# New step lists for the differential-attention layers of a 6-layer transformer kernel

## What is computed

```python
def diff_attention(h, w_in, w_out, ..., sub_g, cos, sin, lambda_init):   # 8 heads, two maps of 64 each
    q, k, v = jnp.split(h @ w_in, [1024, 2048], axis=-1)                 # 256 x 3072
    q = apply_partial_rope(q, cos, sin) * 64 ** -0.5
    k = apply_partial_rope(k, cos, sin)
    s = einsum('bqhcd,bkhcd->bhcqk', q, k)                               # c = 0, 1
    p = softmax(where(causal, s, -inf), axis=-1)
    p = p[:, :, 0] - lam * p[:, :, 1]
    o = einsum('bhqk,bkhe->bqhe', p, v)
    return (rms_norm(o, sub_g) * (1.0 - lambda_init)).reshape(B, S, 1024) @ w_out
```

## Time and profile before

| | us |
|---|---|
| median of 3 runs | 1507.87 (1502.86 to 1507.88) |
| the profiled execution | 1507.24, span 1505.5 |
| TensorE busy in it | 1446.0 (96%), mean granted clock 0.985 |
| VectorE busy | 982.0 (65%) |
| ScalarE busy | 819.4 (54%) |
| mixer of the launch layer (us 11 to 137 of the span) | TensorE's products stand still five times for over 0.1 us |
| mixer of layer 4 (us 889 to 1007) | five times too |
| HBM read | 239.84 MB, 160 GB/s |

### The profile page before, as it was taken

How to read it: one execution, slowest core, us unless ns; L and a number is a source line. 1 busy time by engine, 2 the same in 40 slices (tenths; PEclk the granted TensorE clock), 3 DMA queues, 4 the chain that set the end, 5 groups by cost and what they waited for, 6 DMA issues and landing times.

```text
span 1505.5 us, 19084 instructions
## 1 busy us (share of the span) xinstructions
PE 1446.0 (96%) x7727; PEld 1225.4 (81%) x7727; DVE 982.0 (65%) x1416; ACT 819.4 (54%) x1325; POOL 41.8 (3%) x72
## 2 busy tenths in 40 slices
PE   7999999999999999999999999999999989899988
PEld 6777888888878888887888887778888877788787
DVE  6664665566647655693765567647655698858984
ACT  6675444355535443573543355755443558846883
POOL 3000000000000000000000000000000010102010
PEclk9999999999999999999999999999999999999998
DMA  9343455553434454443445454434454554424430
GB/s 294 116 165 113 168 206 185 185 200 119 168 112 168 172 214 173 155 154 111 169 169 210 181 189 161 168 112 168 169 212 179 175 147 137 168 101 157 144 112 29
DMA packets 119476, 242.13 MB, mean 161 GB/s; under 512 B 3050, under 2 KB 48924, under 8 KB 119388
## 3 DMA queue, kind: packets, MB, share of 16 engines
q1 hardware_dynamic: 117616, 237.25, 44.3%
q0 software_dynamic: 1408, 3.52, 1.0%
q10 hardware_dynamic: 364, 0.13, 0.0%
HBM read 239.84 MB, written 1.05 MB: 160 GB/s over the span
## 4 chain that ended last, share of the span: by engine, by line
PE 78%; DVE 9%; ACT 7%; DMA 4%; issue 1%; SPq 0%; ACTq 0%; DVEq 0%
PE pair L1164 16%; PE pair L1166 15%; PE pair L1165 15%; PE pair L1535 15%; PE pair L1537 8%; DVE wlo L1690 4%; ACT whi L695 3%; PE pair L1357 2%; PE pair L1258 2%; PE pair L1315 2%; DMA raw<-in_diff_w_in 1%; DVE xparts L1726 1%; DMA raw<-in_diff_w_out 1%; ACT xparts L727 1%; PE pair L1336 1%
## 5 line engine op out<-in xcount | busy, mean ns | idle before, releaser
L1690 DVE TENSOR_TENSOR wlo<-raw,whi 128x2048 fp32r<-128x2048 f32 (+2 forms) x240 | 506.3, 2146 | 84.5 <-ACT whi L695 83.7
L695 ACT ACTIVATE whi<-raw 128x2048 fp32r<-128x2048 f32 (+2 forms) x240 | 416.6, 1782 | 90.0 <-DMA raw<-in_mlp_w_down 27.7
L1535 PE MATMUL pair<-xparts,whi 128*128 128x512 f32 x1024 | 260.8, 394 | 7.3 <-DVE xparts L1726 7.1
L1164 PE MATMUL pair<-whi,xparts 128*128 128x512 f32 (+2 forms) x624 | 246.4, 395 | 16.8 <-DVE wlo L1690 8.3
L1164 PE MATMUL pair<-whi,ahi 128*128 128x512 f32 x640 | 254.1, 397 | 0.0
L1166 PE MATMUL pair<-whi,alo 128*128 128x512 f32 x640 | 250.9, 392 | 0.0
L1165 PE MATMUL pair<-wlo,ahi 128*128 128x512 f32 x640 | 250.7, 392 | 0.0
L1166 PE MATMUL pair<-whi,xparts 128*128 128x512 f32 (+2 forms) x624 | 240.6, 386 | 0.0
L1165 PE MATMUL pair<-wlo,xparts 128*128 128x512 f32 (+2 forms) x624 | 239.9, 385 | 0.0
L1535 PEld LDWEIGHTS pair<-xparts,whi 128*128 128x128 f32 x1024 | 184.2, 189 | 44.0 <-issue 6.9
L957 ACT ACTIVATE qkv<-pair 128x512 f32<-128x512 f32 x64 | 38.2, 597 | 274.0 <-PE pair L1537 274.0
(11 more groups left out here) (248 smaller groups left out, 1414.5 us busy)
## 6 DMA issues: line engine op xcount, KB each, us to landing
raw<-in_mlp_w_up SPq DMA_DIRECT2D x32, 2048.0 KB, 8.7
raw<-in_mlp_w_down SPq DMA_DIRECT2D x32, 2048.0 KB, 7.5
raw<-in_diff_w_in SPq DMA_DIRECT2D x22, 1024.0 KB, 7.2
raw<-in_w_in SPq DMA_DIRECT2D x10, 2048.0 KB, 7.8
raw<-in_moba_w_in SPq DMA_DIRECT2D x12, 1024.0 KB, 6.2
raw<-in_diff_w_out SPq DMA_DIRECT2D x4, 2048.0 KB, 7.7
raw<-in_w_uq SPq DMA_DIRECT2D x4, 1152.0 KB, 5.8
raw<-in_moba_w_out SPq DMA_DIRECT2D x2, 2048.0 KB, 8.4
```

Of the source, the lines that this page charges most:

```text
L695: act.activation(whi[:, s, cols], raw[:, s, cols], ACT.Copy).then_inc(*t["hi_split"].one())
L1164: pe.matmul(dst, x_hi, w_hi, start=first, stop=False)
L1535: pe.matmul(pair[f % 2][:, f // 2, :], w_hi[:, k, f * P:(f + 1) * P], xparts[:, k, :, :].rearrange("p a n -> p (a n)"), start=k == 0, stop ...
L1690: dve.tensor_tensor(wlo[:, s, cols], raw[:, s, cols], whi[:, s, cols].bitcast(FP32), ALU.subtract)\
```

## The change

The lists of the differential mixers are drawn anew. No step is added or removed, no step's own instructions change, and the order of blocks, loads and of the slots they use is as it was. `heads`, `scores`, `turn`, `mix` and `features` stand at other places between the eighths of `in` and `out`; on ScalarE and VectorE the two halves of a split are more often apart. TensorE's list in full, and of the other two the lines with the places that matter below (each code line stands 4 lines further down in the new file from L433 on):

```diff
@@ diff_tensor_steps
-            steps = part("in", 0, 0, 8) + part("in", 1, 0, 8) + [("heads", 0)] + part("in", 2, 0, 3)
-            steps += [("scores", 0)] + part("in", 2, 3, 8) + [("turn", 0)] + part("in", 3, 0, 2)
-            steps += [("scores", 1), ("heads", 1), ("mix", 0)] + part("in", 3, 2, 6) + [("turn", 1)] + part("in", 3, 6, 7)
-            steps += [("scores", 2)] + part("in", 3, 7, 8) + part("in", 4, 0, 4) + [("turn", 2), ("heads", 2), ("scores", 3)]
-            steps += part("in", 4, 4, 7) + [("mix", 1)] + part("in", 4, 7, 8) + part("in", 5, 0, 2) + [("turn", 3), ("features", 0)]
-            steps += part("in", 5, 2, 3) + [("scores", 4)] + part("in", 5, 3, 8)
-            steps += [("mix", 2), ("turn", 4), ("mix", 3), ("mix", 4), ("scores", 5), ("heads", 3)]
-            steps += [("features", 1), ("scores", 6)] + part("out", 0, 0, 2) + [("turn", 5)] + part("out", 0, 2, 3) + [("mix", 5)]
-            steps += part("out", 0, 3, 4) + [("scores", 7), ("turn", 6), ("features", 2), ("mix", 6)] + part("out", 0, 4, 6)
-            steps += [("turn", 7)] + part("out", 0, 6, 7) + [("mix", 7)] + part("out", 0, 7, 8) + part("out", 1, 0, 2)
-            steps += [("features", 3)] + part("out", 1, 2, 8)
+            steps = part("in", 0, 0, 8) + part("in", 1, 0, 7) + [("heads", 0)] + part("in", 1, 7, 8)
+            steps += part("in", 2, 0, 2) + [("scores", 0)] + part("in", 2, 2, 7) + [("turn", 0)] + part("in", 2, 7, 8)
+            steps += [("scores", 1)] + part("in", 3, 0, 4) + [("heads", 1)] + part("in", 3, 4, 6) + [("turn", 1)]
+            steps += part("in", 3, 6, 8) + [("mix", 0)] + part("in", 4, 0, 1) + [("scores", 2)] + part("in", 4, 1, 2)
+            steps += [("mix", 1)] + part("in", 4, 2, 3) + [("heads", 2)] + part("in", 4, 3, 4) + [("turn", 2)]
+            steps += part("in", 4, 4, 7) + [("scores", 3)] + part("in", 4, 7, 8) + part("in", 5, 0, 3) + [("turn", 3)]
+            steps += part("in", 5, 3, 4) + [("scores", 4)] + part("in", 5, 4, 5) + [("features", 0)]
+            steps += part("in", 5, 5, 6) + [("mix", 2)] + part("in", 5, 6, 8)
+            steps += [("mix", 3), ("heads", 3), ("turn", 4), ("features", 1), ("scores", 5)]
+            steps += [("mix", 4), ("scores", 6)] + part("out", 0, 0, 2) + [("turn", 5), ("mix", 5), ("scores", 7)]
+            steps += part("out", 0, 2, 4) + [("turn", 6), ("features", 2)] + part("out", 0, 4, 5) + [("mix", 6)]
+            steps += part("out", 0, 5, 6) + [("turn", 7)] + part("out", 0, 6, 7) + [("mix", 7)] + part("out", 0, 7, 8)
+            steps += part("out", 1, 0, 2) + [("features", 3)] + part("out", 1, 2, 8)
@@ diff_scalar_steps
...
-            steps += [("in_results", 1), ("scores", 0), ("split", 0), ("split", 1), ("turn", 0), ("in_results", 2)]
...
-            steps += [("split", 1), ("in_results", 5), ("turn", 4), ("outputs", 1), ("heads", 3), ("features", 1)]
...
+            steps += [("split", 1), ("scores", 0), ("in_results", 1), ("turn", 0), ("in_results", 2)]
...
+            steps += [("in_results", 5), ("outputs", 1), ("heads", 3), ("turn", 4), ("features", 1)]
...
@@ diff_vector_steps
...
-            steps += [("scores", 0), ("turn", 0), ("split", 0), ("split", 1), ("rope", 1), ("scores", 1)]
...
-            steps += [("features", 0), ("scores", 4), ("split", 0), ("turn", 4), ("split", 1), ("rope", 3)]
...
+            steps += [("split", 0), ("scores", 0), ("turn", 0), ("split", 1), ("scores", 1)]
...
+            steps += [("scores", 4), ("turn", 4), ("split", 1), ("features", 0), ("rope", 3)]
...
```

More of the change, by code:

```diff
@@ L414, in diff_scalar_steps @@
-            steps += [("outputs", 0), ("in_results", 4), ("turn", 3), ("features", 0), ("split", 0), ("scores", 4)]
-            steps += [("split", 1), ("in_results", 5), ("turn", 4), ("outputs", 1), ("heads", 3), ("features", 1)]
-            steps += [("scores", 5), ("split", 0), ("split", 1), ("turn", 5), ("scores", 6), ("outputs", 2)]
-            steps += [("turn", 6), ("scores", 7), ("features", 2), ("turn", 7), ("outputs", 3), ("features", 3)]
-            steps += [("out_results", 0)]
+            steps = [("in_results", 0), ("split", 0), ("split", 1), ("heads", 0), ("split", 0)]
@@ new lines, in diff_scalar_steps @@
+            steps += [("split", 1), ("scores", 0), ("in_results", 1), ("turn", 0), ("in_results", 2)]
+            steps += [("split", 0), ("scores", 1), ("split", 1), ("heads", 1), ("split", 0)]
+            steps += [("split", 1), ("turn", 1), ("in_results", 3), ("scores", 2), ("outputs", 0)]
+            steps += [("turn", 2), ("heads", 2), ("split", 0), ("in_results", 4), ("scores", 3)]
+            steps += [("split", 1), ("turn", 3), ("scores", 4), ("split", 0), ("features", 0)]
+            steps += [("in_results", 5), ("outputs", 1), ("heads", 3), ("turn", 4), ("features", 1)]
@@ L419, in diff_scalar_steps @@
+            steps += [("split", 1), ("scores", 5), ("split", 0), ("turn", 5), ("scores", 6)]
+            steps += [("outputs", 2), ("turn", 6), ("scores", 7), ("split", 1), ("turn", 7)]
+            steps += [("out_results", 0), ("features", 2), ("outputs", 3), ("features", 3)]
             return steps
         def diff_vector_steps():
-            steps = [("in_results", 0), ("in_results", 1), ("in_results", 2), ("in_results", 3), ("in_results", 4), ("in_results", 5)]
-            steps += [("split", 0), ("split", 1), ("rope", 0), ("heads", 0), ("split", 0), ("split", 1)]
@@ L425, in diff_vector_steps @@
-            steps += [("scores", 0), ("turn", 0), ("split", 0), ("split", 1), ("rope", 1), ("scores", 1)]
-            steps += [("heads", 1), ("turn", 1), ("split", 0), ("split", 1), ("scores", 2), ("rope", 2)]
-            steps += [("turn", 2), ("heads", 2), ("scores", 3), ("split", 0), ("split", 1), ("turn", 3)]
-            steps += [("features", 0), ("scores", 4), ("split", 0), ("turn", 4), ("split", 1), ("rope", 3)]
-            steps += [("scores", 5), ("heads", 3), ("features", 1), ("turn", 5), ("scores", 6), ("split", 0)]
@@ L430, in diff_vector_steps @@
-            steps += [("split", 1), ("turn", 6), ("scores", 7), ("turn", 7), ("features", 2), ("features", 3)]
-            steps += [("out_results", 0)]
+            steps = [("in_results", 0), ("in_results", 1), ("in_results", 2), ("in_results", 3), ("in_results", 4)]
+            steps += [("in_results", 5), ("rope", 0), ("split", 0), ("heads", 0), ("split", 1)]
+            steps += [("split", 0), ("scores", 0), ("turn", 0), ("split", 1), ("scores", 1)]
+            steps += [("rope", 1), ("split", 0), ("out_results", 0), ("turn", 1), ("split", 1)]
@@ new lines, in diff_vector_steps @@
+            steps += [("heads", 1), ("scores", 2), ("rope", 2), ("turn", 2), ("split", 0)]
+            steps += [("split", 1), ("heads", 2), ("scores", 3), ("turn", 3), ("split", 0)]
+            steps += [("scores", 4), ("turn", 4), ("split", 1), ("features", 0), ("rope", 3)]
+            steps += [("split", 0), ("heads", 3), ("scores", 5), ("features", 1), ("scores", 6)]
+            steps += [("turn", 5), ("split", 1), ("scores", 7), ("turn", 6), ("turn", 7)]
+            steps += [("split", 0), ("features", 2), ("features", 3), ("split", 1)]
```

3 lines of the change are left out of this document (removed).

## The result

| | before | after |
|---|---|---|
| median of 5 runs each, us | 1507.80 (1502.86 to 1507.88) | 1497.66 (1494.62 to 1499.20) |
| ratio, 95% interval | | 0.9948 [0.9932, 0.9964] |
| the profiled execution, us | 1507.24, span 1505.5 | 1497.7, span 1495.9 |
| mean granted clock in it | 0.985 | 0.987 |

The forecast was 1502.4 with a range from 1497.5 to 1507.5. With 0.52% it is just in the class "faster by over 0.5%" (chance 0.33), and its interval reaches down to 0.36%.

What follows compares the result with a forecast made beforehand. TensorE was taken as the bound, busy 1446.0 of 1505.5 us, so only its losses could be won. Launch layer -4.25 and layer 4 -0.6, together -4.85 from 1507.24, gave 1502.4 us, range 1497.5 to 1507.5.

Steps and rivals of the forecast that it cites:

- The launch copy: Launch layer: TensorE waits 0.55 us instead of 3.46 in front of `in 3` for ScalarE's copy; -2.9 us.
- The clock at launch: Launch layer: the half-clock stretch behind the wait at `in 3` goes away; -2.5 us.
- the resumptions: Both mixers: block products interrupted 23 times instead of 17, five more counted here at 0.13 us; +0.65 us per layer.
- the steps no longer second: Both mixers: three steps that stood second in a run now follow block products, saving about 0.1 each; -0.3 us.
- `heads 1` in layer 4: Layer 4: the rope comes about 2.5 us before `heads 1` wants it, so its wait goes; -2.0 us.
- The closing run: Run after `in 5`: ends at 8.5 us; with `mix 2` moved into `in 5` at 0.7, net +0.55 layer 4, +0.3 launch.
- Behind the closing run: After each closing run: waits at `mix 5` and `out 0` make 1.5 us against 1.0; +0.5 us per layer.
- The clock behind the closing runs: Both layers: low stretches costing about 1.5 us each stay, as the new run holds as much waiting; 0.
- the rival, around which its lower edge was drawn: Both layers: the low stretches behind the closing runs go too, 3.0 us less, giving 1499.4 us; chance 0.25.
- the rival at launch: Launch layer: the low stretch behind `in 3`'s wait stays, as the skill's rule has it; +2.5, 1504.9 us; chance 0.08.
- longer low stretch: Closing runs, both layers: low clock costs 2.5 us each, 1504.4 (chance 0.12), or grows by 3.7 each, 1509.8 (chance 0.05).
- the tight margin of `turn 1` and `turn 3`: Possible failure at these steps; at launch, ScalarE and VectorE work fits before `turn 1` by a few tenths of a us.

Runs made afterwards that it cites:

- Experiment 3: Changed kernel with both halves of block 4's split back in front of `in_results 2` on ScalarE; 1503.15 us, ratio 0.998.
- Experiment 7: Changed kernel with three short steps put next to others on TensorE, 20 interruptions of block products instead of 23; 1500.04 us, ratio 0.9958.
- experiment 1: Changed kernel's order up to the end of `in 5`, then the closing run and tail of before; 1501.26 us, ratio 0.9973.
- experiment 5: Changed lists in the launch layer only, layer 4 with the lists of before; 1500.17 us, ratio 0.9954.
- experiment 6: Changed kernel with VectorE taking `scores 5` before the low part of `heads 3`; 1504.80 us, ratio 0.9991.
- experiment 4: Changed kernel with the first eighth of `out 0` moved between `mix 3` and `heads 3` on TensorE; 1497.34 us, ratio 0.9944.
- experiment 8: Same steps as the changed kernel, in lists searched by walking all three engines with measured durations; 1489.13 us, ratio 0.9887.
- experiment 2: Order of before up to `in 5`, then the changed kernel's closing run and tail; 1505.28 us, ratio 0.9994.

## Why the prediction was right and wrong

**The launch copy (-2.9): right.** TensorE's idle time there fell from 3.46 to about 0.3 us, 3.15, and `in 3` started at 2.24 against the 2.4 worked out. Experiment 3 brings it back with one split.

**The clock at launch (-2.5): right.** The low stretch is gone. Experiment 3 prices wait and clock together at 5.47 from `in 1` on, for 5.4 forecast. Up to the closing run the launch layer won 4.96 us (88.94 to 83.98 from its first product). The forecast for that part was -4.35, or -4.7 without the resumptions net of the steps no longer second.

**`heads 1` in layer 4 (-2.0) and the resumptions (+0.65 -0.3): the first right, the second wrong.** No wait is left at `heads 1`. From 892.52 to the closing run layer 4 won 1.25 us (77.14 to 75.89). The forecast for this was -0.95, made of -2.0, 0.7 for `mix 2` and the 0.35 net for resumptions. Without the latter it would be -1.3. Experiment 7 points to the reason: joining three steps saved 0.0 in a stretch of 42.73 us. So the 0.12 us read from the earlier trace rows seem to go with the step, and not with the number of interruptions; that is shown for three joins in layer 4 only.

**The closing run: right.** It was worked out at 8.5 us and took 8.46 in both layers (8.66 and 8.90 before). The idle times in it are 1.64, 0.47 and 0.64 where 1.9, 0.6 and 1.0 were named. Those were counted from the end of the work, while the rows' idle begins only when TensorE's last rows are out; the starts agree within 0.15 us (`heads 3` at 2.47 for 2.5, `features 1` at 4.36 for 4.35, `scores 5` at 5.65 for 5.8).

**Behind the closing run (+0.5 each): too much.** The stretch from there to `features 3` fell by 1.03 us at launch (20.79 to 19.76) and by 1.30 in layer 4 (21.01 to 19.71). With 1.5 each from the clock, that leaves +0.5 and +0.2, so the term was near at launch and 0.3 too large in layer 4.

**The clock behind the closing runs (0): wrong, and the step that failed.** This is -1.5 in each layer, 3.0 of the 4.7 us that the forecast missed. The argument was that the new run holds as much waiting as the old. By the rows it holds more: TensorE's idle times in the closing runs of before are 0.26 and 1.75 us at launch and 0.18 and 1.67 in layer 4, 2.01 and 1.85 together, and those of after are 2.75 in both.

```profile
102.14 0.91 PE L1357 MATMUL pair<-qkv,pT 128*128 128x128 f32 x6 [0.26 <-ACT pT L899]
...
107.81 0.38 PE L1315 MATMUL pair<-qk_hi 64*128 64x256 f32 x2 [1.75 <-DVE qk_lo L1899]
```

The clock was low behind the shorter sums and full behind the longer one, so the sum is not what the chip went by. Over all kernels there were 22 closing runs, each seen in one execution. In 7 of them the last short step before the products, `scores 6`, waited 1.61 to 1.87 us: before (2), experiment 1 (2), layer 4 of experiment 5 (1) and experiment 6 (2). The clock was low behind 6 of those 7, and behind none of the 15 others. That it isn't the length of a wait by itself is shown by after: 1.64 us in front of `heads 3`, 6 us before the products, with full clock (as the 1.73 in front of `heads 1` in before), while 1.61 us in front of `scores 6` in experiment 5 had the low clock behind it. That it isn't transposes in place of products is shown by the same run: from 962.5 to 967.35 TensorE does only transposes and waits. Experiment 6 moved only VectorE's order and brought the low stretches back, in both layers. But it added idle time too, and no kernel here moved a wait at an unchanged sum. Experiment 1, with the same wait at launch and no low stretch, shows that the place makes it likely and doesn't decide it.

Nor is a wait close to the block products enough. At the start of the launch layer `in 1` waits for a low part, directly in front of its products and with nothing but products before it. In nine traces it waited 0.74 to 2.61 us there and full clock followed, in after for one; the 2.78 us of experiment 6 was followed by 3.4 us of low clock, and the 3.74 of experiment 5 by 6.8. After, and in experiment 6:

```profile
26.76 0.50 PE L1168 MATMUL pair<-whi,xparts 128*128 128x512 f32 x1 [2.61 <-DVE wlo L1694]
```

```profile
26.48 0.50 PE L1168 MATMUL pair<-whi,xparts 128*128 128x512 f32 x1 [2.78 <-DVE wlo L1694]
```

So what stood before the wait counts too: behind block products no low clock followed 2.61 us, at the end of a run of short steps one followed 1.61. What the chip looks at stays open. That the measured time still lies in the range is due to the rival, around which its lower edge was drawn, and not to the sum: the sum's own bounds ended at 1500.6.

The Trainium skill (TensorE: Matmul & The Clock Gate, section "HAM oscillation") describes a low clock for each group of products that follows a wait. The waits it tells of are of 3 to 5 us. The traces agree where waits were about that long: behind those of 2.91, 3.18, 3.21 and 3.74 us directly in front of products the clock was low each time. The section says nothing of shorter ones, neither of the 0.55 us that the prediction left in front of `in 3`, so it did not support the rival at launch, nor of the 1.61 to 1.87 us that were followed by a low clock here in 6 of 7 cases.

**The other rivals.** The launch stretch did not stay, and the closing runs got no longer low stretch. The doubt about the tight margin of `turn 1` and `turn 3` was not needed: no wait stands there.

**The whole miss.** The two layers gave 9.16 us where 4.85 were forecast. Of the 4.3 between, 3.0 are the clock, 0.7 the resumptions in both layers, 0.3 the launch copy and 0.3 the stretch behind layer 4's closing run. Outside the two layers another 0.7 us came off, and the first product started 0.27 later (11.38 for 11.11), which no step of the change accounts for: the part behind layer 4 alone varies from 491 to 498 us over the kernels.

## What to carry to other kernels

Filling one wait inside a chain over three engines is not enough: walk all three lists with the measured durations, and see where the time comes out again (experiment 4, one wait filled on one engine: nothing gained; experiment 8, all three lists drawn anew: 6.7 us less over the two layers than the changed kernel). Where a wait must remain in a run of short steps, put it in front of an early step and not in front of the last one before the products: here the first cost its own length, and the second cost 1.5 us more in clock 6 times of 7. Price the parts of such a change by distances between starts of the same instruction in both traces, since total times of single executions differed here by as much as the change was worth. Even then look at what lies inside the distance: `in 0` alone differed by up to 1.6 us between executions with one list.

## What the runs showed of the hardware

The wait in front of `in 3` was followed by 6.8 us of low clock in before (3.21 us) and in experiment 3 (2.91), and by 3.4 in experiment 2 (3.18). So the price of a lost clock can't be read off the wait: it was a low stretch of 3.4 us, which cost 1.5 behind the closing runs, or one of 6.8, which cost 2.5 at launch. A wait of 2.61 us between block products had no low clock behind it (after, us 26.76), one of 1.61 us at the end of a run of short steps had (experiment 5, layer 4). And joining three short steps, so that block products of 128x512 are interrupted 20 times and not 23, saved 0.0 us in 42.73.
